# Two encoder layers on one core: token groups staggered through both layers, weight differences all on VectorE, MLP visits written out

## What is computed

```python
for i in range(DEPTH):
    if i % N_MIXERS == 0:
        y, nh = short_conv_mixer(x, conv_states[j], a_w_in[j], a_conv_w[j], a_w_out[j])
    else:
        y, nh = pool_mixer(x, pool_states[j], pos0, b_w_grp[j], b_scale[j])
    h = layer_norm(ALPHA * x + y, ln1_g[i], ln1_b[i])
    r = jax.nn.relu(h @ mlp_w1[i])
    f = (r * r) @ mlp_w2[i]
    e = (p[i] @ ple_w[i]) * jax.nn.sigmoid(h @ ple_gate_w[i])
    x = layer_norm(ALPHA * h + f + e, ln2_g[i], ln2_b[i])
```

## Time and profile before

| what | value |
| --- | --- |
| time, median of 3 runs | 2262.23 us (2260.36 to 2270.69) |
| span of the profiled execution | 2252.7 us |
| TensorE busy | 2141.2 us, 95% |
| VectorE, ScalarE, GpSimd busy | 1208.0, 779.1, 261.4 us |
| granted TensorE clock, mean | 0.982 |

### The profile page before, as it was taken

The page is one execution under the profiler, slowest core; times in us unless marked ns, Lnnn a source line. Parts: engine busy times, 40 slices in busy tenths (PEclk is TensorE's granted clock), DMA queues, the critical chain, the costliest instruction groups (busy, mean ns, idle before and its releaser), DMA issues.

```text
span 2252.7 us, 32406 instructions
## 1 busy us (share of the span) xinstructions
PE 2141.2 (95%) x13166; PEld 2120.1 (94%) x13166; DVE 1208.0 (54%) x1721; ACT 779.1 (35%) x1203; POOL 261.4 (12%) x135
## 2 busy tenths in 40 slices
PE   8999999899999999999998988789999999999987
PEld 8999999899999999999898987679999999999986
DVE  4333368853344344444667879895343434443487
ACT  3222224532223222324343554353233233223354
POOL 0000000100000000003123125310011110001120
PEclk9999999999999999999999998899999999999998
DMA  4011142321211111114311233233122121112232
GB/s 164 29 56 56 37 131 85 100 90 56 64 38 47 47 39 54 42 51 131 113 53 50 88 119 85 66 98 104 57 66 66 59 73 57 38 56 76 75 113 96
DMA packets 47402, 164.68 MB, mean 73 GB/s; under 512 B 7488, under 2 KB 7616, under 8 KB 47296
## 3 DMA queue, kind: packets, MB, share of 16 engines
q1 hardware_dynamic: 45216, 163.04, 22.9%
q10 hardware_dynamic: 2080, 0.12, 0.1%
HBM read 158.68 MB, written 4.46 MB: 72 GB/s over the span
## 4 chain that ended last, share of the span: by engine, by line
PE 81%; DVE 14%; ACT 3%; issue 2%; DMA 0%; ACTq 0%; DVEq 0%
PE ps L645 27%; PE ps L646 26%; PE ps L647 26%; DVE w_split L571 2%; ACT w_split L750 1%; DVE ln_squares L960 1%; DVE ln_squares L959 1%; DVE acc L1070 1%; DVE acc L1007 1%; DVE acc L990 1%; DVE h_hi L1029 1%; DVE std L999 1%; DVE r_lo L1066 1%; DVE win L1023 1%; ACT acc L809 1%
## 5 line engine op out<-in xcount | busy, mean ns | idle before, releaser
L645 PE MATMUL ps<-h_hi,w_split 128*128 128x352 f32 x2160 | 701.1, 325 | 22.4 <-DVE w_split L571 9.3
L647 PE MATMUL ps<-h_hi,w_split 128*128 128x352 f32 x2160 | 694.0, 321 | 0.0
L646 PE MATMUL ps<-h_lo,w_split 128*128 128x352 f32 x2160 | 693.9, 321 | 0.0
L645 PE MATMUL ps<-r_hi,w_split 128*128 128x352 f32 x1632 | 540.8, 331 | 44.0 <-DVE acc L1070 42.3
L646 PE MATMUL ps<-r_lo,w_split 128*128 128x352 f32 x1632 | 529.3, 324 | 0.0
L647 PE MATMUL ps<-r_hi,w_split 128*128 128x352 f32 x1632 | 529.0, 324 | 0.0
L1070 DVE TENSOR_TENSOR acc<-acc,ps 128x352 f32<-128x352 f32 x768 | 377.8, 518 | 170.3 <-PE ps L647 168.9
L645 PEld LDWEIGHTS ps<-h_hi,w_split 128*128 128x128 f32 x2160 | 406.6, 188 | 26.2 <-DVE w_split L571 12.1
L646 PEld LDWEIGHTS ps<-h_lo,w_split 128*128 128x128 f32 x2160 | 407.9, 189 | 0.4
L647 PEld LDWEIGHTS ps<-h_hi,w_split 128*128 128x128 f32 x2160 | 406.4, 188 | 0.0
L1066 DVE TENSOR_TENSOR r_lo<-t,r_hi 128x352 fp32r<-128x352 f32 x192 | 116.4, 608 | 507.5 <-ACT r_hi L870 507.4
(11 more groups left out here) (81 smaller groups left out, 1286.1 us busy)
## 6 DMA issues: line engine op xcount, KB each, us to landing
w_raw<-w_stream SPq DMA_DIRECT2D x290, 512.0 KB, 3.7
x_raw<-x_t SPq DMA_DIRECT2D x6, 704.0 KB, 8.3
y_t<-acc SPq DMA_DIRECT2D x4, 704.0 KB, 4.8
w_raw<-p_t SPq DMA_DIRECT2D x6, 352.0 KB, 3.0
y_t<-acc SPq DMA_DIRECT2D x4, 352.0 KB, 2.2
pool_new<-acc ACTq DMA_DIRECT2D x2, 60.0 KB, 6.1
vec<-vectors SPq DMA_DIRECT2D x1, 78.0 KB, 7.3
pool_history<-pool_hist SPq DMA_DIRECT2D x1, 60.0 KB, 6.8
```

Source lines behind the costliest of these rows:

```text
L645: pe.matmul(out, wh, mov_h, start=first, stop=False)
L646: pe.matmul(out, wh, mov_l, start=False, stop=False)
L647: return pe.matmul(out, wl, mov_h, start=False, stop=last)
```

## The change

The values are the same and so is the number of matmuls. Three things differ.

**Order.** `LEAD` replaces `AHEAD` and `BEHIND`. In each layer group 0 goes through the gate and runs alone for 5 visits (9 in the second layer), then group 1 passes its gate and both run for 3 (5), then group 2 passes its gate, all three run for the rest, then groups 1 and 2 for 5 (9) visits, then group 2 alone for 3 (5). So each group finishes a layer in a stretch of its own. Gate weights are streamed three times per layer, not twice; 28 units more are loaded in all, 318 where there were 290.

**Placement.** `beside` places each part of a norm or pooling at the first step where `room` says that VectorE has time left in three steps. The two `grp` products of a window now stand in one step. `give_slots` hands a freed weight slot to the next unit in order of need.

**Differences.** All are made on VectorE: the 74 that GpSimd made, and those of the 28 new units. The loops over visits are written out.

```diff
-AHEAD = (2, 5, 8)
-BEHIND = 5
-ALONE, PAIR, ALL = (0,), (1, 2), (0, 1, 2)
+LEAD = (5, 3), (9, 5)
 
 NORMS = [("mix", 0, 0), ("mix", 0, 1), ("mix", 0, 2),
-         ("mlp", 0, 0), ("mix", 1, 0), ("mlp", 0, 1), ("mlp", 0, 2), ("mix", 1, 1), ("mix", 1, 2),
+         ("mlp", 0, 0), ("mix", 1, 0), ("mlp", 0, 1), ("mix", 1, 1), ("mlp", 0, 2), ("mix", 1, 2),
          ("mlp", 1, 0), ("mlp", 1, 1), ("mlp", 1, 2)]
+
+SLOTS = 4
+MM_US, ADD_US, GATE_US, R_LO_US, SPLIT_US = 0.159, 0.52, 0.57, 0.61, 1.23
 
 
 @dataclass
@@ -52,16 +53,7 @@
...
+def give_slots(plan, stays):
...
+    freed = sorted(range(len(stays)), key=lambda i: stays[i][2])
+    slots = {}
+    for i, (name, begin, end) in enumerate(stays):
+        if i < SLOTS:
+            slots[i] = i
+        else:
+            gone = freed[i - SLOTS]
+            slots[i] = slots[gone]
+            at = stays[gone][2]
+            assert at < begin, (name, at, begin)
+            if plan[at].kind == "up" and plan[at].mm == CHUNK - 1 and plan[at + 1].kind == "down" and at + 1 < begin:
+                at += 1
+            conds = [("b_full", plan[at].b + len(plan[at].blocks))] if plan[at].kind == "down" and at == stays[gone][2] else []
+            plan[at].refill.append((name, slots[i], conds))
+        plan[begin].need.append(slots[i])
...
-        def splitter(v, j):
-            return "dve" if todo[v][1] == ALL or v in (0, swap) else by(j)
...
-            if v == loop_at:
...
+    def room(step):
+
+        own = len(step.refill) * SPLIT_US
+        if step.kind == "down":
+            return 24 * MM_US - own - 4 * ADD_US
+        if step.kind == "up":
+            return 24 * MM_US - own - R_LO_US
+        if step.kind == "gate":
+            return 30 * MM_US - own - 2 * GATE_US
+        return 24 * MM_US - own - 2 * ADD_US
...
+    def norm(i, done):
 
         n = NORMS.index(i)
-        rows = {0: [("sum", n, done)], 2: [("mean", n)], 3: [("square", n)], 4: [("vsum", n)], 6: [("var", n)], 7: [("rstd", n)],
-                9: [("norm", n)], 10: [("affine", n, 0)], 11: [("affine", n, 1)]}
+        rows = [(0, 3.2, [("sum", n, done)]), (2, 3.1, [("mean", n)]), (1, 0, [("square", n)]), (1, 3.2, [("vsum", n)]), (2, 0.6, [("var", n)]),
+                (1, 4.0, [("rstd", n)]), (1, 3.1, [("norm", n)]), (1, 0, [("affine", n, 0)]), (1, 0, [("affine", n, 1)])]
         if i[0] == "mix":
-            rows.update({12: [("hi", n)], lo: [("lo", n)]})
+            rows += [(1, 0, [("hi", n)]), (1, 3.1, [("lo", n)])]
...
     def pooling(n):
-
-        rows = {}
-        for q, (fill, centre) in enumerate(((0, 2), (2, 4), (4, 6), (5, 8))):
-            rows.setdefault(fill, []).append(("fill", 4 * n + q))
-            rows.setdefault(centre, []).append(("centre", 4 * n + q))
-            for j in range(2):
-                rows.setdefault(centre + j + 3, []).append(("gadd", 8 * n + 2 * q + j))
-                rows.setdefault(centre + j + 2, []).append(("grp", 8 * n + 2 * q + j, 4 + q // 2))
+        rows = [(1, 0, [("fill", 4 * n)]), (1, 0, [("fill", 4 * n + 1)])]
+        for q in range(len(WINDOWS)):
+            rows.append((1, 3.0, [("centre", 4 * n + q)]))
+            if q + 2 < len(WINDOWS):
+                rows.append((0, 0, [("fill", 4 * n + q + 2)]))
+            if q:
+                rows.append((1, 1.1, [("grp", 8 * n + 2 * q - 2 + j, 4 + (q - 1) // 2) for j in range(2)]
+                             + [("gadd", 8 * n + 2 * q - 2 + j) for j in range(2)]))
+        rows.append((2, 1.1, [("grp", 8 * n + 6 + j, 5) for j in range(2)] + [("gadd", 8 * n + 6 + j) for j in range(2)]))
         return rows
...
+    def beside(first, *chains, grp_from=0):
+
+
+        steps = [s for s in plan[first:] if s.kind not in ("ple", "refill")]
+        at = 0
+        for row in (row for chain in chains for row in chain):
+            gap, cost, parts = row
+            at += gap
+            while parts[0][0] == "grp" and plan.index(steps[at]) <= grp_from:
+                at += 1
+            while cost and sum(left[id(s)] for s in steps[at:at + 3]) < cost:
+                at += 1
+            steps[at].side += parts
+            for s in steps[at:at + 3]:
+                spent = min(cost, max(left[id(s)], 0))
+                left[id(s)] -= spent
+                cost -= spent
+        return plan.index(steps[at])
...
+    marks = {}
+    for layer in range(DEPTH):
+        alone, pair = LEAD[layer]
+        gates(layer, 0)
+        marks["gates", layer, 0] = len(plan)
+        visits(layer, [(c, (0,)) for c in range(alone)])
+        marks["before", layer, 1] = len(plan)
+        gates(layer, 1)
+        marks["gates", layer, 1] = len(plan)
+        visits(layer, [(c, (0, 1)) for c in range(alone, alone + pair)])
+        marks["before", layer, 2] = len(plan)
+        gates(layer, 2)
+        marks["gates", layer, 2] = len(plan)
+        visits(layer, [(c, (0, 1, 2)) for c in range(alone + pair, NCH)] + [(c, (1, 2)) for c in range(alone)]
+               + [(c, (2,)) for c in range(alone, alone + pair)])
+        marks["end", layer] = len(plan)
...
+    for n in range(NG):
+        begin, done = last_down(0, n)
+        at = beside(max(begin, at), norm(("mlp", 0, n), done), pooling(n), grp_from=grp_from)
+        ple_loads(at + 1, 1, [("grp_full", 8 * (n + 1))])
+        at = beside(at, norm(("mix", 1, n), ("y_added", 8 * (n + 1))))
+        limit = marks["end", 0] if n == 0 else marks["before", 1, n]
+        assert at < limit, (n, at, limit)
+        if n < NG - 1:
+            grp_loads(*ple_end(1, n))
+            grp_from = ple_end(1, n)[0] + 3
...
-        def walk(eng, steps, do):
-
+            ins.then_inc(w_lo, 1)
+
+        def walk(steps, do):
             for step in steps:
-                if step.kind == "loop":
-                    with eng.Fori(0, step.passes) as i:
-                        for inner in step.body:
-                            do(inner.later(i))
-                else:
-                    do(step)
+                do(step)
...
-                for u, slot, _ in step.refill:
-                    if u.by == "pool":
-                        pool.wait_ge(w_hi, u.s + 1)
-                        subtract_hi(pool, u, slot)
```

More of the change, by code:

```diff
@@ L125, in unit @@
         total[0] += 1
-        last_in[q] = u
+        in_raw[q] = u
         return u
-    first = [unit(("in", m, j), "dve", j) for m in range(KD) for j in range(3)][:3]
+    first = [unit(("in", m, j), j) for m in range(KD) for j in range(3)][:3]
     for j in range(3):
[L131 to L136, removed]
-            if step.kind == "loop":
[L138 to L150, removed]
@@ L173, in add @@
         return plan[-1]
-    def refill(step, name, slot, conds=(), by="dve"):
-        if name is not None:
-            step.refill.append((name, slot, list(conds), by))
-    def inputs(layer, groups):
-        for n, part in zip(groups, sorted(range(NG), key=lambda part: r_used.get(part, 0))):
-            held[n] = part
-            users = [step for step in plan if step.kind == "down" and step.part == part]
-            last, conds = (users[-1], [("b_full", r_used[part])]) if users else (outputs_done, [("out_added", NG * KD)])
-            refill(last, ("p", layer, n), ("p", part), conds)
@@ L188, in quads, with stay, use, refill @@
-    def quads(groups, emit, names, following, by):
+    def stay(name):
+        stays.append([name, None, None])
+        return len(stays) - 1
+    def use(step, *which):
+        for i in which:
+            step.units.append(i)
+            at = len(plan) - 1
+            stays[i][1] = at if stays[i][1] is None else stays[i][1]
+            stays[i][2] = at
+    def refill(step, name, slot, conds=()):
+        step.refill.append((name, slot, list(conds)))
+    def token_inputs(layer, n):
+        part = min(range(NG), key=lambda part: r_used.get(part, 0))
+        held[n] = part
+        users = [step for step in plan if step.kind == "down" and step.part == part]
+        last, conds = (users[-1], [("b_full", r_used[part])]) if users else (outputs_done, [("out_added", NG * KD)])
+        refill(last, ("p", layer, n), ("p", part), conds)
@@ L398, in make_plan @@
[L398 to L405 removed]
+    outs((0,))
+    outs((1, 2))
+    outputs_done = add("refill")
@@ new lines, in make_plan, with grp_loads, ple_loads @@
+    add("rest").side.append(("finish", NORMS.index(("mlp", 1, 2))))
+    for step in [s for s in plan if s.kind == "down"][-2:]:
+        step.final = True
+    def grp_loads(at, b_done):
+        for j in range(2):
+            refill(plan[at], ("grp", j), 4 + j, [("b_full", b_done)])
+    def ple_loads(at, layer, conds):
+        for j in range(KP):
+            refill(plan[at], ("ple", layer, j), 4 + j, conds)
+    left = {}
+    give_slots(plan, stays)
+    out3 = [("out", 3), 3, []]
+    start.refill.append(tuple(out3))
@@ new lines, in make_plan, with ple_end, last_down @@
+    ple_loads(0, 0, conv_done)
+    for step in plan:
+        left[id(step)] = room(step)
```

(13 more changed lines are left out.)

250 lines of the change are left out of this document (74 added, 176 removed).

## The result

The changed kernel takes 2225.98 us (median of 4 runs, 2224.69 to 2227.51) against 2261.3 for the kernel before in the same session: ratio 0.9841, 95% interval 0.9812 to 0.9871. It is faster, by 35 us or 1.6%, and the interval leaves out 1. I had forecast 2175, with 2145 to 2220 for the range; the time lies outside it, and the gain is two fifths of the 87 us that I had worked out.

What follows compares the result with a forecast made beforehand. TensorE bounds four fifths of the time, VectorE the 425 us around the layer change. Gains of 128 and 1.5 less 6.7, 6, 17 and 13 give 87 us: span 2166, plus 9.5 makes 2175 us, range 2145 to 2220.

Steps and rivals of the forecast that it cites:

- The bound: Whole kernel: TensorE bounds four fifths of the time, VectorE the 425 us around the layer change; TensorE loses 128 us.
- The order, step by step: Layer change: norms and poolings fit at 60 to 90% of VectorE, at most 3 us late at first `down` steps.
- The residue of 13 us: Loss still left in the 750 us of stretches carrying norms or poolings in the changed order; taken as 13 us.
- the pair wait: Second `grp` product of a window waits for ScalarE to scale the first in their shared PSUM bank; 12 waits, 17 us.
- 6.7, 6: Losses that stay: 6.7 us of waits at 288.7 and the end, 6 us of slower float32 norm matmuls.
- My upper bound of 44: Most that the 750 us carrying norms or poolings would lose, at the rate of 283 to 540 us: 44 us.
- The differences: 102 more weight differences on VectorE, 125 us more work, cost nothing directly; less GpSimd slowdown, gain counted inside the 128 us.
- The 9.5 us between span and median: Added to the forecast span of 2166 us to give the forecast median of 2175 us.
- The loops: Unrolling the two loops over visits removes a wait at each entry, some 1.5 us in all.
- Dense stretches as dear as before: Rival: 750 us with VectorE 60 to 90% busy lose more than 44 us; 2206 to 2250 us, chance 0.14.
- Late weights: Rival: alone-visit and gate weight units come late behind VectorE pieces, making it slower; chance 0.09 with anything else above 2273.
- The signs that I had told: Signs of being wrong: `w_split` waits on VectorE, `acc` waits of 4 us and more, clock under 0.97 in the middle.

Runs made afterwards that it cites:

- A: Changed kernel with no piece of over 2 us of VectorE work at the second up step of a pair; 2194.98 us, ratio 0.9688.
- C: Changed kernel with ScalarE's window copy (`fill`) placed one step behind the centring, after the pair of `grp` products; 2217.13 us, ratio 0.9796.
- the three edits together: Changed kernel with no long VectorE piece at second up steps, `fill` behind the centring, no norm scaling or cast at first up steps; 2175.66 us, ratio 0.9634.
- D: Changed kernel with no scaling or cast of a norm on ScalarE at the first up step of a pair; 2213.76 us, ratio 0.9814.
- B: Changed kernel with the two `grp` products of a window in separate steps, each followed by its own addition; 2205.33 us, ratio 0.9755.

## Why the prediction was wrong

**The bound.** Right. TensorE's count is the floor and VectorE's and ScalarE's lateness the rest. The pace of 0.1587 us held in every undisturbed stage of the changed kernel; in those of A, C and the three edits together it was 0.161 in some of them (see C).

**The order, step by step: this step failed.** I wrote that "at no first `down` step does VectorE start more than 3 us late". In that walk, and in the plan's own costs, a piece began as soon as VectorE's running sum was free. In the kernel it begins behind the step's `r_lo`, which waits for three instructions of ScalarE. So a piece of 3 to 4 us at a second `up` step can end past the 3.8 us that four banks hold, 5.2 us into the `down` blocks in the timeline above, however much room VectorE has on average; nine times it did. The run with edit A shows it: 29 us of span. The same walk had no ScalarE in it (`room` counts VectorE's time alone); edit D shows what that queue costs at one place, and C at two.

**The residue of 13 us.** It is this step's term, and I had named it the least trusted. I took the value near nothing; the term was 57 us too small together with what the pair wait had extra. Less 6.7, 6 and 25.0 for the pairs, the 100 us lost leave 62 where I had 13. 30.3 of them are waits for additions; 18.3 are 136 matmuls after 283 us that start 0.25 to 0.35 us apart instead of 0.159, so at the lower clock; of the remaining 13, some 3 are shorter waits (2.1 at L1015, 0.7 for `w_split`, 0.5 others), and the rest I have not traced. My upper bound of 44 was too low as well: I took one stage's rate, 15 us in 257, for the worst that a spaced order could do, and 1500 to 1700 lost 40 in 200.

**The pair wait.** The mechanism was right: 11 waits, where I had 12. Nine of them sum to 13.6 us, 1.5 each against my mean of 1.4. The term of 17 measured 25.0 because of two waits of 5.6 and 5.7 for the window copy, and edit C takes just those away. I had worked the price out from ScalarE's arithmetic alone, without what else is queued there and can block.

**The differences.** Right. 102 more of them cost nothing visible on TensorE, and `r_lo` fell to 531 ns. This part alone, in the old order, is worth some 12 us. VectorE came to 1255.6 us, not 1290, as more of its other instructions grew shorter than I had reckoned (last section).

**The 9.5 us between span and median.** They do not lie around the span, as I had it: in every later execution time and span are 1.7 to 1.9 us apart (2226.73 and 2224.9 in the profiled one). The profiled execution of the kernel before, 2252.7, was some 8 us faster than its median. So by the spans I miss 59 us, by the times 51.

**The loops.** Right in size, 1.5 us forecast and nothing measured, and wrong in the reading: the wait taken for the loop's is not the loop's.

**The rivals.** "Dense stretches as dear as before" named the right range (2206 to 2250) and in part the right cause, "a late piece delays a whole chain over four engines"; but it tied the price to VectorE's fullness, and the runs show the loss where VectorE is 60% busy and not where it is 77%. I had given it 0.14. Late weights did not come: 0.7 us outside the start. The signs that I had told did their work: the clock went under 0.97 and there were waits above 4 us.

By parts: the differences alone give 12 us, the written-out loops none, so the order and the placement with its pairs of products give about 23 by subtraction, if the parts add. How they would do alone, with GpSimd still splitting, was not run, and neither was a kernel that moves the window sums off GpSimd.

## What to carry to other kernels

When you walk a schedule by a running sum, let each piece start when the instruction ahead of it on its engine can finish, not when the engine's sum of work is free; then ask whether the piece ends before the banks downstream are full. Put long pieces behind a step's late input only where nothing short-buffered follows. A wait that is put down to one engine may belong to the engine that this one was idle for: look at the releaser's own idle time before you make it faster. And in a queue that holds its order, work that is free but waits for a buffer belongs behind the work that someone waits for.

## What the runs showed of the hardware

**The clock after a wait.** The granted clock went down after the longest waits, and that cost up to a third of what the waits did (18.3 us beside 55.3 of waits for additions and scalings). In the changed kernel, around 1537.33 (wait of 5.46 us) and 1558.13 (5.75 us), the first matmul behind the wait takes 0.63 us, and the next 15 or so start 0.29 to 0.30 us apart; then the pace of 0.16 is back. The stage:

```profile
1550.00:1600.00 50.00, 40.19 (x224) 39.16 (x224) 28.81 (x49) 14.27 (x27) 9.80 (x6) 0.90 0.14 42
```

The lower pace is that of the lower of the two clock levels (1.2 against 2.4 GHz). The waits of 2.88 us at 1628.71 and 3.30 at 1668.76 were followed by it too. Of the sixteen waits of 1.2 to 2.4 us between 283 and 2200, four were (1.87 at 1067.14 and 2.14 at 1368.14, for two), and twelve were not (1.88 at 1184.74 and 2.14 at 1348.60, for two). With A, C and D together no wait in this part is above 2.14 us, and 1500 to 1600 holds this, against 483 matmuls at 0.91 in the changed kernel:

```profile
1500.00:1600.00 100.00, 92.41 (x572) 90.61 (x571) 67.16 (x110) 44.06 (x81) 14.99 (x10) 1.00 0.27 76
```

Matmuls at the lower pace after 283 us, without the program's last 20: 151 in the kernel before (20.3 us lost), 136 in the changed one (18.3), 95 with A (12.7), 115 with D (15.4), 37 with A, C and D (4.9). So these edits gained more than the waits. But B has 142 (18.9) and C 144 (19.2), though both took the waits of 5.6 and 5.7 us for `y_scaled_t` away: more of their short waits were followed by the lower pace (five of thirteen and six of fourteen). Over the ten profiled executions 49 of the 51 waits of more than 2.8 us were followed by it, outside the start and the end; the two that were not (3.50 us at 1177.40 and 2.92 at 1495.01) are in the kernel before with its visits written out. So a long wait nearly always brings the lower clock here; what decides it behind a short one the rows do not show, and a wait of chosen length was not tried by itself.

**How much GpSimd slows VectorE.** 102 differences more are 126 us, but VectorE's busy time rose by 48 only. Its other instructions, the same in number, shape and operation, lost 78 us: `r_lo` 116.4 to 101.9, and in the kernel before and after

```profile
L1029 DVE CAST h_hi<-win 128x704 fp32r<-128x704 f32 (+2 forms) x16 | 20.8, 1320 | 0.4
L961 DVE TENSOR_TENSOR sum_mean<-ln_squares 128x352 f32<-128x352 f32 x11 | 15.2, 1379 | 0.4
```

```profile
L995 DVE CAST h_hi<-win 128x704 fp32r<-128x704 f32 (+2 forms) x16 | 7.7, 501 | 0.4
L927 DVE TENSOR_TENSOR sum_mean<-ln_squares 128x352 f32<-128x352 f32 x11 | 5.8, 525 | 0.4
```

I had named this slowdown and not its size. What GpSimd's differences alone cost shows in the kernel before with all of them on VectorE: they are 93 us more there (323.8 less 230.9), and VectorE's busy time rose by 29, so the others lost some 63. The other 15 of the 78 came with the new order. So a difference on VectorE (1.23 us) is much cheaper than on GpSimd, whose 189 us cost VectorE some 63 while they relieved it of 93.
